# Attention in a streaming encoder step: the value products of a query row issued in one burst behind the step's scores and transposes

## The chip, the cores and the metric

The kernel runs on one core of one Trainium2 chip. The metric is the device time of one execution in microseconds (us). Three runs of the kernel before gave 3194.82, 3190.05 and 3192.64 us, so the median is 3192.64 us.

## The reference, cut to what matters

One layer of a hybrid encoder is computed for 2048 prompt frames and 32 sample frames: a mixer (projections and an RWKV recurrence), attention, an output projection with routing, a mixture of experts and a final normalization. The change is in the attention alone. For each of 8 heads, with blocks of 128 queries, it computes

```
s = q_nope . k_nope + q_pe . k_pe          # 96 channels
s = where(key chunk <= query chunk, s * MLA_SCALE, -inf)   # chunks of 64
p = softmax(s)                             # over all keys up to the query's block
out = p . v                                # 64 channels a head
```

All is float32.

## The kernel before, in words

Function `attention` (line 1265) works on two heads at a time (h = 0 and 1), so it makes four turns, one for each pair of heads. A turn first computes keys (L1546) and values (L1555) from the latents, ten groups in all, and then walks over 17 query rows j of 128 queries. Row j needs j + 1 key blocks; `groups(j)` (L1276) cuts them into groups of up to four blocks, so rows 0 to 3 have one group, rows 4 to 7 two, rows 8 to 11 three, rows 12 to 15 four. Row 16 holds the sample frames and has one group. A chunk is one group of one head: `chunks` (L1282) lists 82 of them in the order row, head, group. Chunk n goes through these stages:

- **scores** (L1491): TensorE multiplies queries by up to 512 keys into one of five PSUM banks (instruction L1497).
- **maxima** (L1582): VectorE takes the row maximum (L1593, the masked corner in L1589 or L1592); when the chunk is the last of its head in the row it also joins and scales the maxima (L1596, L1597).
- **exp** (L1469, corner L1472): ScalarE exponentiates. It needs the joined maximum of the row and head, so no chunk of a head can start before that head's last chunk has its maximum.
- **transposes** (L1500): TensorE turns the probabilities, up to four 128x128 blocks (L1509), into one of two PSUM banks (5 and 6).
- **copy**: VectorE copies the bank to one of 14 SBUF slots of `PT` (L1640).
- **value products** (`values`, L1512): for each pair of a row and a key block, both heads' products are accumulated in bank 7 (L1528). One such pair is four matmul records in the trace. The first product of row j waits for the output of row j - 1 (`out_{j-1}`), because both use bank 7.
- **row_sum** (L1599): VectorE adds the row sums of a head, inverts them and spreads them to 64 columns (L1602, L1603, L1609, tile `wide`). **row_rec** (L1534, called recT in the code) is one TensorE transpose of `wide` (L1537); it needs `wide` of both heads. ScalarE copies it out (L1482), and **output** (L1611) multiplies bank 7 by it (L1615).

The order is written out by hand. Every engine runs through numbered steps n and keeps its own program order. In step n TensorE issues `scores(n + 4)`, then the value products that the table `share` gives to the step, then `row_rec` if a row ends here (`row_end`), then `transposes(n)` (L1564 to L1572). VectorE issues `maxima(n + 4)`, then `row_sum` of chunk n - 2 where that is a head's last chunk, then `output` of the row that ended in step n - 1, then the copy of chunk n (L1625 to L1643). ScalarE issues `exp(n)`, then the copy of the row's reciprocals if a row ended in step n - 1.

The planner (L1295 to L1306) places each pair of a row and a key block not earlier than LAG = 3 steps after the second head's chunk of its group, with at most BURST = 3 pairs in a step, and starts a row at least two steps after the end of the row before:

```python
step = max(step, place[j, 1, g] + LAG, free)
while share.get(step, 0) == BURST:
    step += 1
```

A turn has 138 pairs. By this rule they fall into 52 steps of one to three pairs. For example, row 13 (14 pairs) is spread over five steps, and row 8 (9 pairs) over three.

Of the kernel before, what the change touches and what calls it, by code (L numbers as in the profile page):

```python
# [33 lines left out]
NT = SEQ // P + 1  # L34
# [1230 lines left out]
def attention(nc, io, scr):  # L1265
# [3 lines left out]
    KT = SEQ // P + 2  # L1269
    attnT = transposed_out(scr)  # L1270
    AHEAD, SB, TB = 4, 5, 2
    LAG = 3
    NP, NPT = 4, 14
    BURST = 3

    def groups(j):  # L1276
        if j == NT - 1:
# [5 lines left out]
    count = len(chunks)  # L1283
# [7 lines left out]
    def ends(n):  # L1291
        return n == count - 1 or chunks[n + 1][:2] != chunks[n][:2]
# [1 line left out]

    pairs = [(j, g, s) for j in range(NT) for g in range(len(groups(j))) for s in range(groups(j)[g][1])]  # L1295
    share, row_end = {}, {}
    step, free = 0, 0
    for i, (j, g, s) in enumerate(pairs):
        step = max(step, place[j, 1, g] + LAG, free)
        while share.get(step, 0) == BURST:  # L1300
            step += 1
        share[step] = share.get(step, 0) + 1
        if i + 1 == len(pairs) or pairs[i + 1][0] != j:
            row_end[step] = j
            free = step + 2
    steps = max(max(share) + 1, count)  # L1306
    last_use = {n: max(m for m in range(count) if m % NP == n % NP) for n in range(NP)}

    def in_order(ahead, before, at, after):
        names = [x for n in range(min(AHEAD, count)) for x in ahead(n)]  # L1310
        for n in range(steps):
            names += ahead(n + AHEAD) if n + AHEAD < count else []
            names += before(n) + (at(n) if n < count else []) + after(n)
        return names
# [14 lines left out]
        return [f"max{n}"] + ([f"rowmax{j}_{h}", f"negmax{j}_{h}"] if ends(n) else [])  # L1329

    def sum_names(n):
        if n < LAG - 1 or n - LAG + 1 >= count or not ends(n - LAG + 1):
            return []
        j, h, g = chunks[n - LAG + 1]
        return [f"sum{j}_{h}", f"sum_rec{j}_{h}", f"rec_wide{j}_{h}"]

    def out_names(n):
# [1 line left out]

    KV = [f"K{n}" for n in range(5)]  # L1340
    VV = [f"V{n}" for n in range(5)]
    ten_names = KV + VV + in_order(lambda n: [f"S{n}"], pv_names, lambda n: [f"PT{n}"], none)
    vec_names = VV + in_order(max_names, lambda n: sum_names(n) + out_names(n), lambda n: [f"PT{n}"], none)
    vec_names += out_names(steps)
    act_names = KV + [x for n in range(steps + 1) for x in
# [3 lines left out]
    with ExitStack() as ctx:  # L1349
# [136 lines left out]
        @block.tensor  # L1486
        def _(pe):
            pe.wait_ge(latents.sem, latents.done(0))
            pe.wait_ge(setup, 6)

            def scores(t, n):  # L1491
                j, h, gi = chunks[n]
                k0 = groups(j)[gi][0]
                wd, _ = width(n)
                if n >= SB:
                    t.w(act, f"exp{n - SB}")
                t.mark(pe.matmul(bank[n % SB][:, 0:wd], qT[h][keys(h), j * P:(j + 1) * P],  # L1497
                                 kT[h][keys(h), k0 * P:k0 * P + wd], start=True, stop=True), f"S{n}")

            def transposes(t, n):  # L1500
                wd, corner = width(n)
                t.w(act, f"exp{n}")
                if n >= TB:
                    t.w(vec, f"PT{n - TB}")
                if corner:
                    t.w(pol, f"corner{n}")
                for c in range(0, wd, P):
                    rows = min(P, wd - c)
                    ins = pe.transpose(bank[SB + n % TB][0:rows, c:c + P], PQ[:, n % NP, c:c + rows], ident[:, :])  # L1509
                t.mark(ins, f"PT{n}")  # L1510

            def values(t):  # L1512

                for j in range(NT):
                    gs = groups(j)
                    for gi, (k0, k, last) in enumerate(gs):
                        m0, m1 = place[j, 0, gi], place[j, 1, gi]
                        t.w(vec, f"PT{m1}")
                        if gi == 0:
                            if j > 0:  # L1520
                                t.w(vec, f"out_{j - 1}")
                            else:
                                t.w0(vec, last_out)
                        for s in range(k):
                            rows = last if s == k - 1 else P
                            end = gi == len(gs) - 1 and s == k - 1
                            for h, m in ((0, m0), (1, m1)):
                                ins = pe.matmul(bank[7][64 * h:64 * h + 64, 0:P], vals[0:rows, k0 + s, 64 * h:64 * h + 64],  # L1528
                                                PT[0:rows, m % NPT, s, :], start=(gi == 0 and s == 0), stop=end)
                            if s == k - 1:  # L1530
                                t.mark(ins, f"PV{j}_{gi}")
                            yield

            def row_rec(t, j):  # L1534

                t.w(vec, f"rec_wide{j}_1")
                t.mark(pe.transpose(bank[7][:, P:2 * P], wide[:].rearrange("p a n -> p (a n)"), ident[:, :]), f"recT{j}")  # L1537

            def turn(t):
                t.arrived(w_in)  # L1540
                t.w0(vec, last_out)
                t.w0(act, f"exp{count - 1}")
                for n in range(5):
                    wd = min(512, KT * P - 512 * n)
                    for c in range(CKV):
                        ins = pe.matmul(bank[n][:, 0:wd], w[:, c, 0:P], lat[:, c, 512 * n:512 * n + wd],  # L1546
                                        start=(c == 0), stop=(c == CKV - 1))
                    t.mark(ins, f"K{n}")
                for n in range(5):
                    b = bank[5 + n % 3]  # L1550
                    if n >= 3:
                        t.w(vec, f"V{n - 3}")
                    for k in range(4 * n, min(4 * n + 4, KT)):
                        for c in range(CKV):
                            ins = pe.matmul(b[:, (k % 4) * P:(k % 4 + 1) * P], lat[:, c, k * P:(k + 1) * P],  # L1555
                                            w[:, c, P:2 * P], start=(c == 0), stop=(c == CKV - 1))
                    t.mark(ins, f"V{n}")
                t.w(act, "K4")
                t.w(vec, "V4")
                t.arrived(q_in)  # L1560
                for n in range(AHEAD):
                    scores(t, n)
                v = values(t)
                for n in range(steps):  # L1564
                    if n + AHEAD < count:
                        scores(t, n + AHEAD)
                    for _ in range(share.get(n, 0)):
                        next(v)
                    if n in row_end:
                        row_rec(t, row_end[n])  # L1570
                    if n < count:
                        transposes(t, n)  # L1572
                for _ in v:
                    pass

            engine_loop(pe, ten, turns, turn)

        @block.vector
        def _(v):
# [37 lines left out]
            def turn(t):  # L1617
# [7 lines left out]
                for n in range(steps + 1):  # L1625
                    if n + AHEAD < count:
                        maxima(t, n + AHEAD)
                    if sum_names(n):
                        row_sum(t, n - LAG + 1)
                    if n - 1 in row_end:  # L1630
                        output(t, row_end[n - 1])
                    if n < count:
# [976 lines left out]
```

How the kernel before makes its waits and increments, by code:

```python
    def _wait(self, counts, name, turn):  # L199
        v = self.known.get((counts.sem.name, name, turn))
        if v is None:
            v = counts.done(self.i + turn, name) if name else counts.done(self.i + turn)
        self.eng.wait_ge(counts.sem, v)
# [1 line left out]
    def do(self, ins, name):  # L205
        self.own.mark(ins, name)
        self.eng.wait_ge(self.own.sem, self.own.done(self.i, name))
# [314 lines left out]
        @block.sync  # L523
# [11 lines left out]
                consts.go(sp.dma_start(w_wa[hs], io["w_wa"][hs, 512 * r:512 * r + 512]))  # L535
                consts.go(sp.dma_start(cst[hs], io["cst"].rearrange("p (a n) -> p a n", a=7)[hs, :, hs]))
                consts.go(sp.dma_start(one64[hs], io["ident"][hs, hs]))
                consts.go(sp.dma_start(levs[hs], io["levs"].rearrange("p (a n) -> p a n", a=LEVELS)
                                      [hs, 0:LEVELS - 1, 32 * r:32 * r + 32]))
            consts.go(sp.dma_start(w_g[:], io["w_g"]))
            for k in (1, 0, 2):
                c0, c1 = w_cols[k]
                sp.dma_start(w_in[:, :, c0:c1], w_src[:, :, c0:c1]).then_inc(w_part[k], 16)
            sp.dma_start(w_uq[:], io["w_uq"].rearrange("p (a n) -> p a n", a=CQ)).then_inc(w_queries, 16)
            sp.wait_ge(first_x, 2)
            def x_load(tile):
# [91 lines left out]
            for d in (mla_out, rwkv_out, edge_out, state_out):  # L640
                sp.wait_ge(d.sem, d.done(NT - 1))
            sp.wait_ge(x_in.sem, x_in.done(NT + 1))
# [805 lines left out]
        @block.scalar  # L1448
        def _(a):
            a.wait_ge(setup, 6)
            def turn(t):
```

## Time and profile before

| what | value |
|---|---|
| median of three runs | 3192.64 us |
| span of the profiled execution, first to last instruction | 3185.8 us |
| TensorE matmul busy over the span | 2883.6 us (91%) |
| VectorE busy over the span | 1738.2 us (55%) |
| mean granted TensorE clock | 0.965 of full speed |
| attention with its setup, all four turns | about 1378 to 2075 us from the span's start |

The profile of one execution gives no total beside its span; the 6.8 us between the span and the median lie around the span or between executions. In timelines a line gives the start in us, the duration in us, the engine, the line of the code, the operation, its output and inputs, and the count that is merged; a bracket at the end gives how long the engine stood idle before it and what released it. Ends of matmuls are modelled, so the distance from one start to the next start is the better measure of TensorE's time. In the four turns the first scores start at 1396.58, 1570.82, 1743.95 and 1917.87 us, and the turns follow each other in the same pattern, so the first turn is read.

### The profile page before, as it was taken

What the parts mean: (1) busy time and instruction counts of PE and PEld (TensorE: products, weight loads), DVE (VectorE), ACT (ScalarE), POOL (GpSimd) and SP (SyncE); (2) the same over time, 40 slices, a digit from 0 to 9 for tenths busy, and PEclk for the clock granted to TensorE, in tenths of its full rate; (3) what the DMA queues carried; (4) which work ended last, traced back from release to release, by engine and by line L of the source; (5) the groups of instructions that cost most, each with busy time, mean ns of one, the idle gap of its engine ahead of it and who ended that gap; (6) DMA issues with size and microseconds to landing.
All of it is one profiled execution on the core that took longest, in us unless ns stands there. A gap on an engine that the chain in (4) does not pass through costs nothing. (4 is left out here: it accounts for less than half of the span.)

```text
span 3185.8 us, 65923 instructions
## 1 busy us (share of the span) xinstructions
PE 2883.6 (91%) x26600; PEld 2202.1 (69%) x26600; DVE 1738.2 (55%) x3821; ACT 970.2 (30%) x2497; POOL 522.3 (16%) x554
## 2 busy tenths in 40 slices
PE   7999999999999999669899898989976999999990
PEld 6888888888888888545555555545545777777770
DVE  1666666666666666558686868822235222222225
ACT  2333333333333333234343434412220111111116
POOL 0000000000000000010000000011113554545540
PEclk9999999999999999689999999999988999999995
DMA  6211111222111211420101010033335899886447
GB/s 196 37 38 37 37 37 38 40 39 39 37 38 39 42 38 37 93 88 1 39 1 39 1 36 1 1 127 132 126 110 210 282 336 325 278 279 177 97 93 251
DMA packets 337225, 310.23 MB, mean 97 GB/s; under 512 B 235200, under 2 KB 290528, under 8 KB 322528
## 3 DMA queue, kind: packets, MB, share of 16 engines
q1 hardware_dynamic: 315424, 238.88, 24.5%
q0 software_dynamic: 21504, 67.13, 9.1%
q8 instruction: 218, 3.57, 0.5%
q14 instruction: 79, 0.65, 0.1%
HBM read 208.12 MB, written 84.42 MB: 92 GB/s over the span
## 5 line engine op out<-in xcount | busy, mean ns | idle before, releaser
L814 PE MATMUL mx_bank<-mx_xT,mx_w_in 128*128 128x128 f32 x5168 | 646.4, 281 | 16.9 <-DVEq L281 13.4
L814 PEld LDWEIGHTS mx_bank<-mx_xT,mx_w_in 128*128 128x128 f32 x5168 | 600.8, 193 | 60.5 <-issue 36.2
L2311 DVE STREAM_TRANSPOSE ex_xT<-ex_x 128x256 f32<-128x256 f32 x256 | 141.5, 610 | 332.3 <-DMA ex_x<-scr_hx,ex_idx 332.3
L1497 PE MATMUL at_bank<-pl_kT,pl_qT 128*128 128x512 f32 (+5 forms) x656 | 289.9, 528 | 2.3 <-issue 2.3
L1469 ACT ACTIVATE at_PQ<-at_bank,at_nms 128x512 f32<-128x512 f32 (+5 forms) x328 | 192.7, 595 | 252.9 <-DVE at_nms L1597 251.5
L2159 POOL DMA_INDIRECT ex_x<-scr_hx,ex_idx x256 | 244.9, 957 | 114.8 <-issue 77.7
L2242 PE MATMUL ex_gate<-pl_wg,ex_xT 128*128 x1024 | 233.6, 381 | 13.7 <-DVE ex_xT L2311 11.4
L2242 PEld LDWEIGHTS ex_gate<-pl_wg,ex_xT 128*128 128x128 f32 x1024 | 195.1, 191 | 68.7 <-issue 44.9
L2266 PE MATMUL ex_down<-pl_wd,ex_hT 128*128 x512 | 230.3, 592 | 1.5 <-ACT ex_hT L2194 1.5
L2242 PE MATMUL ex_up<-pl_wu,ex_xT 128*128 x1024 | 231.6, 379 | 0.0
L1528 PEld LDWEIGHTS at_bank<-at_PT,at_vals 128*64 128x64 f32 (+1 forms) x2208 | 117.4, 136 | 151.5 <-issue 78.1
L1640 DVE COPY at_PT<-at_bank 128x512 f32<-128x512 f32 (+3 forms) x328 | 196.4, 600 | 44.6 <-PE at_bank L1509 28.1
L2242 PEld LDWEIGHTS ex_up<-pl_wu,ex_xT 128*128 128x128 f32 x1024 | 190.2, 191 | 23.1
L2202 ACT ACTIVATE ex_y<-ex_down,kept_onehot 128x512 f32<-128x512 f32 x128 | 81.0, 684 | 410.6 <-PE ex_down L2266 410.6
L1509 PE MATMUL at_bank<-pl_at_ident,at_PQ 128*128 128x128 f32 x1104 | 184.9, 282 | 22.5 <-ACT at_PQ L1469 11.7
L710 ACT ACTIVATE mx_pr<-mx_bank 128x256 f32<-128x256 f32 (+1 forms) x68 | 36.7, 540 | 553.3 <-PE mx_bank L814 471.7
L1509 PEld LDWEIGHTS at_bank<-pl_at_ident,at_PQ 128*128 128x128 f32 x1104 | 126.4, 141 | 107.2 <-issue 44.6
L1593 DVE TENSOR_REDUCE at_mx<-at_bank 128x1 f32<-128x512 f32 (+5 forms) x328 | 188.6, 575 | 15.9 <-PE at_bank L1497 10.5
L1528 PE MATMUL at_bank<-at_PT,at_vals 128*64 128x128 f32 (+1 forms) x2208 | 165.8, 282 | 26.1 <-DVE at_o_sb L1615 26.1
L665 POOL TENSOR_TENSOR mx_AR<-mx_u,mx_ep 128x512 f32<-128x512 f32 x17 | 20.1, 1181 | 1000.2 <-DVE mx_kh L1154 1000.2
L2266 PEld LDWEIGHTS ex_down<-pl_wd,ex_hT 128*128 128x128 f32 x512 | 97.2, 190 | 96.8 <-issue 93.6
L2170 POOL DMA_INDIRECT scr_acc<-ex_y,kept_tokens x64 | 103.3, 1615 | 271.1 <-ACT ex_y L2202 128.9
(310 smaller groups left out, 4480.2 us busy)
## 6 DMA issues: line engine op xcount, KB each, us to landing
pl_wg<-in_w_eg SPq DMA_DIRECT2D x32, 1024.0 KB, 6.1
pl_wu<-in_w_eu SPq DMA_DIRECT2D x32, 1024.0 KB, 10.3
pl_wd<-in_w_ed SPq DMA_DIRECT2D x32, 1024.0 KB, 14.3
mx_x<-in_x SPq DMA_DIRECT2D x76, 128.0 KB, 3.7
pl_ro_x<-in_x SPq DMA_DIRECT2D x17, 512.0 KB, 4.2
scr_hx<-ro_h SPq DMA_DIRECT2D x17, 512.0 KB, 2.6
scr_acc<-ro_ha SPq DMA_DIRECT2D x17, 512.0 KB, 3.1
co_r<-scr_acc SPq DMA_DIRECT2D x17, 512.0 KB, 5.6
```

Of the source, the lines that this page charges most:

```text
L814: ins = pe.matmul(dst, w_in[:, k, col:col + n], xT[:, k, :], start=(k == 0), stop=(k == KC - 1))
L1469: ins = a.activation(PQ[:, n % NP, 0:full], b[:, 0:full], ACT.Exp, bias=bias, scale=SCALE, accum_out=sums[:, j, h, 1 + gi:2 + gi])
L1497: t.mark(pe.matmul(bank[n % SB][:, 0:wd], qT[h][keys(h), j * P:(j + 1) * P], kT[h][keys(h), k0 * P:k0 * P + wd], start=True, stop=True), f ...
L1509: ins = pe.transpose(bank[SB + n % TB][0:rows, c:c + P], PQ[:, n % NP, c:c + rows], ident[:, :])
L1528: ins = pe.matmul(bank[7][64 * h:64 * h + 64, 0:P], vals[0:rows, k0 + s, 64 * h:64 * h + 64], PT[0:rows, m % NPT, s, :], start=(gi == 0 an ...
L1593: t.do(v.tensor_reduce(mx[:, 1 + gi:2 + gi], b[:, 0:wd], AX.X, ALU.max), f"max{n}")
L1640: ins = v.tensor_copy(PT[:, n % NPT, 0:full, :], b[:, 0:full * P].rearrange("p (a n) -> p a n", a=full))
L2159: x_in[s].go(g.indirect_dma_start(x[s][:, k, :], None, rows, bass.IndirectOffsetOnAxis(ap=idx[:, at:at + 1], axis=0)))
L2170: y_add[s].go(g.indirect_dma_start(scr["acc"], bass.IndirectOffsetOnAxis(ap=tokens[:, at:at + 1], axis=0), y[s][:], None, compute_op=ALU.add))
L2242: ins = pe.matmul(b[s][:, 0:FE], xT[s][:, k, :], wv[:, k * FE:(k + 1) * FE], start=(k == 0), stop=(k == KC - 1))
L2266: ins = pe.matmul(down_b[n][:, :], hT[s][:, m, :], wv[:, m * D + n * 512:m * D + (n + 1) * 512], start=(m == 0), stop=(m == FC - 1))
L2311: ins = v.transpose(xT[s][:, :, 32 * h:32 * h + 32], x[s][:, h, :].rearrange("p (i k) -> p k i", k=KC))
```

## The change

The planner places whole rows. A row with one, two or three groups has all its value products in one step, LAG = 2 steps after the last chunk of the row; a row with four groups has two such steps, one for its first two groups (8 pairs), one for the rest. In the step the value products now come behind the transposes. The number of the chunk whose sum VectorE takes in step n stays n - 2.

```diff
-    LAG = 3
+    LAG = 2
     NP, NPT = 4, 14
-    BURST = 3
...
-    step, free = 0, 0
-    for i, (j, g, s) in enumerate(pairs):
-        step = max(step, place[j, 1, g] + LAG, free)
-        while share.get(step, 0) == BURST:
-            step += 1
-        share[step] = share.get(step, 0) + 1
-        if i + 1 == len(pairs) or pairs[i + 1][0] != j:
-            row_end[step] = j
-            free = step + 2
+    free = 0
+    for j in range(NT):
+        gs = groups(j)
+        parts = ((0, 1), (2, 3)) if len(gs) == 4 else (tuple(range(len(gs))),)
+        for part in parts:
+            step = max(place[j, 1, part[-1]] + LAG, free)
+            assert step not in share
+            share[step] = sum(gs[g][1] for g in part)
+            free = step + 1
+        row_end[step] = j
+        free = step + 2
...
-        if n < LAG - 1 or n - LAG + 1 >= count or not ends(n - LAG + 1):
+        if n < LAG or n - LAG >= count or not ends(n - LAG):
...
                     if n + AHEAD < count:
                         scores(t, n + AHEAD)
+                    if n < count:
+                        transposes(t, n)
                     for _ in range(share.get(n, 0)):
                         next(v)
                     if n in row_end:
                         row_rec(t, row_end[n])
-                    if n < count:
-                        transposes(t, n)
...
-                        row_sum(t, n - LAG + 1)
+                        row_sum(t, n - LAG)
```

A turn then has 21 steps with value products instead of 52. They are steps 3, 5, 7 and 9 (rows 0 to 3, 1 to 4 pairs), 13, 17, 21 and 25 (rows 4 to 7, 5 to 8 pairs), 31, 37, 43 and 49 (rows 8 to 11, 9 to 12 pairs), 55 and 57, 63 and 65, 71 and 73, 79 and 81 (rows 12 to 15, 8 pairs and then 5 to 8), and 83 (row 16, 2 pairs). Before, rows 0 to 15 ended in steps 4, 6, 8, 11, 14, 18, 23, 27, 32, 39, 45, 51, 59, 67, 75 and 84.

## Rows read from the trace of the kernel before

**Rows 1.** The profile's page: span, and busy time of two engines

```profile
span 3185.8 us, 65923 instructions
...
PE 2883.6 (91%) x26600; PEld 2202.1 (69%) x26600; DVE 1738.2 (55%) x3821; ACT 970.2 (30%) x2497; POOL 522.3 (16%) x554
```

**Rows 2.** Busy time by stretch: bounds, us, PE, PEld, DVE, ACT, POOL, clock, DMA, GB/s

```profile
1396.60:1443.60 47.00, 39.45 (x247) 23.21 (x248) 41.81 (x150) 22.98 (x87) 3.69 (x13) 0.96 0.03 7
1443.60:1485.30 41.70, 40.42 (x291) 24.49 (x290) 36.10 (x99) 19.14 (x69) 1.99 (x7) 1.00 0.00 1
1485.30:1539.80 54.50, 51.88 (x379) 30.28 (x377) 44.58 (x109) 21.16 (x74) 1.99 (x7) 1.00 0.00 1
1539.80:1552.70 12.90, 9.37 (x101) 6.62 (x99) 8.47 (x32) 4.68 (x17) 1.35 (x5) 0.99 0.56 131
...
1412.00:1416.00 4.00, 4.00 (x19) 2.50 (x19) 3.64 (x15) 1.75 (x7) 0.28 (x1) 0.57 0.00 0
```

**Rows 3.** VectorE's timeline, first 47 us: its two longer waits

```profile
1421.60 0.69 DVE L1640 COPY at_PT<-at_bank 128x512 f32<-128x512 f32 x1 [0.92 <-PE at_bank L1509]
...
1428.60 0.69 DVE L1640 COPY at_PT<-at_bank 128x512 f32<-128x512 f32 x1 [0.41 <-DVE at_mx L1593]
```

**Rows 4.** TensorE's timeline: a step without value products, one with three pairs

```profile
1471.90 1.02 PE L1497 MATMUL at_bank<-pl_kT,pl_qT 96*128 96x512 f32 x2
...
1473.20 1.02 PE L1497 MATMUL at_bank<-pl_kT,pl_qT 128*128 128x512 f32 x2
...
1476.64 1.02 PE L1497 MATMUL at_bank<-pl_kT,pl_qT 128*128 128x512 f32 x2
...
1478.90 1.02 PE L1497 MATMUL at_bank<-pl_kT,pl_qT 96*128 96x512 f32 x2
```

**Rows 5.** TensorE's timeline: a burst of one pair, transposes ahead of value products

```profile
1442.64 0.44 PE L1528 MATMUL at_bank<-at_PT,at_vals 128*64 128x128 f32 x4
1443.01 0.33 PE L1537 MATMUL at_bank<-pl_at_ident,at_wide 128*128 128x128 f32 x1
...
1542.61 0.63 PE L1509 MATMUL at_bank<-pl_at_ident,at_PQ 128*128 128x128 f32 x4 [0.51 <-DVE at_PT L1640]
```

**Rows 6.** Timeline of all engines, turn's end: TensorE's longest burst

```profile
1543.17 0.88 PE L1528 MATMUL at_bank<-at_PT,at_vals 128*64 128x128 f32 x12
...
1547.60 1.75 PE L1528 MATMUL at_bank<-at_PT,at_vals 128*64 128x128 f32 x28
...
1549.28 0.33 PE L1537 MATMUL at_bank<-pl_at_ident,at_wide 128*128 128x128 f32 x1
```

**Rows 7.** VectorE's timeline: reciprocals of rows 1 and 5, and the next full maximum

```profile
1410.80 0.26 DVE L1609 TENSOR_SCALAR at_wide<-at_ones,at_rec 128x64 f32<-128x64 f32 x1
...
1411.63 0.68 DVE L1593 TENSOR_REDUCE at_mx<-at_bank 128x1 f32<-128x512 f32 x1
...
1434.41 0.25 DVE L1609 TENSOR_SCALAR at_wide<-at_ones,at_rec 128x64 f32<-128x64 f32 x1
...
1435.05 0.68 DVE L1593 TENSOR_REDUCE at_mx<-at_bank 128x1 f32<-128x512 f32 x1
```

**Rows 8.** Timeline of all engines, steps 67 and 68: a head's chain

```profile
1522.48 0.81 PE L1497 MATMUL at_bank<-pl_kT,pl_qT 128*128 128x384 f32 x2
...
1524.61 0.69 ACT L1469 ACTIVATE at_PQ<-at_bank,at_nms 128x512 f32<-128x512 f32 x1 [4.92 <-DVE at_nms L1597]
...
1525.44 0.66 PE L1509 MATMUL at_bank<-pl_at_ident,at_PQ 128*128 128x128 f32 x4
```

**Rows 9.** TensorE's timeline: waits for row 6's output and for an exp

```profile
1446.58 0.88 PE L1528 MATMUL at_bank<-at_PT,at_vals 128*64 128x128 f32 x12 [1.28 <-DVE at_o_sb L1615]
...
1488.38 0.66 PE L1509 MATMUL at_bank<-pl_at_ident,at_PQ 128*128 128x128 f32 x4 [1.30 <-ACT at_PQ L1469]
```

**Rows 10.** TensorE's timeline inside the stretch of lower clock

```profile
1413.95 1.91 PE L1497 MATMUL at_bank<-pl_kT,pl_qT 96*128 96x512 f32 x2
```

More of the change, by code:

```diff
@@ L1331, in sum_names @@
     def sum_names(n):
-        if n < LAG - 1 or n - LAG + 1 >= count or not ends(n - LAG + 1):
+        if n < LAG or n - LAG >= count or not ends(n - LAG):
             return []
-        j, h, g = chunks[n - LAG + 1]
+        j, h, g = chunks[n - LAG]
         return [f"sum{j}_{h}", f"sum_rec{j}_{h}", f"rec_wide{j}_{h}"]
@@ L1341, in attention @@
     VV = [f"V{n}" for n in range(5)]
-    ten_names = KV + VV + in_order(lambda n: [f"S{n}"], pv_names, lambda n: [f"PT{n}"], none)
+    ten_names = KV + VV + in_order(lambda n: [f"S{n}"], none, lambda n: [f"PT{n}"], pv_names)
     vec_names = VV + in_order(max_names, lambda n: sum_names(n) + out_names(n), lambda n: [f"PT{n}"], none)
```

## The prediction

> **What bounds the kernel now.** The page comes first: TensorE is busy 91% of the span, VectorE 55% [rows 1]. That is an average over stages; the change touches only the part of attention in which chunks are processed, four times some 156 us. I therefore cut the first turn by the rows that are worked on. Rows 0 to 7 (steps 0 to 23) take 47.0 us, with VectorE busy 41.81 us in 150 instructions [rows 2]. Its timeline has only two idle gaps worth the name there, 0.92 and 0.41 us [rows 3]; the rest of the difference are hundredths between its instructions. So VectorE is the bound of the short rows. In rows 8 to 11 (41.7 us) and in steps 48 to 75 (54.5 us) it is TensorE: busy 40.42 and 51.88 us, against 36.10 and 44.58 for VectorE [rows 2].
>
> **What TensorE pays for a burst.** A full step without value products takes 1473.20 - 1471.90 = 1.30 us from scores to scores, one with three pairs 1478.90 - 1476.64 = 2.26 us [rows 4]. So three pairs cost 0.96 us. One pair takes 0.37 us from its first product to the reciprocals' transpose [rows 5], seven pairs 1.68 us [rows 6]: a pair costs (1.68 - 0.37) / 6 = 0.218 us. Three pairs are 0.65 us of work, and 0.31 us is the price of a burst as such, the two switches of operand shape. Behind transposes the entry takes 1543.17 - 1542.61 = 0.56 us [rows 5, 6], where four transposes ahead of scores take 0.44 (1.30 less 0.86 for the scores), so 0.12 us. The exit into scores doesn't occur in this trace. Its nearest row is the exit into the reciprocals' transpose, 0.37 - 0.22 = 0.15 us, and I add 0.07 us for the slower first weights, which gives 0.34 us a burst; the bounds are 0.2 and 0.5 us, or 3 us either way in a turn of 21 bursts.
>
> **The parts of the change, per turn.** The operations stay the same in number and shape, and no DMA moves. 52 bursts become 21. If TensorE were the bound throughout, that would give 52 x 0.31 - 21 x 0.34 = 9.0 us a turn. What remains of it, stretch by stretch:
>
> *Rows 0 to 7: loss.* Here the order matters, not the count. VectorE forms the reciprocals of a row in step n by chunk n - 2, as before. TensorE's transpose of them stood one step later; now, with LAG = 2, it stands in the same step n, ahead of scores n + 5. Behind the waiting transpose are queued those scores, for which VectorE waits in its next step. Before, they were already in their bank. VectorE is behind TensorE here, so the wait is real. Take row 1: the reciprocals end at 1410.80 + 0.26 = 1411.06 and the next full maximum started at 1411.63 [rows 7]. Now the transpose (0.07 us to reach it, 0.17 us itself) and the scores (1.02 us, 0.08 us to VectorE) lie between: 1411.06 + 1.34 = 1412.40, which is 0.77 us later. Row 5: 1434.66 + 1.34 = 1436.00 against 1435.05, 0.95 us. The other six row ends read in the same way give 1.10, 0.47, 1.02, 1.09, 0.08 (a narrow chunk) and 0.82 us, and the 0.92 and 0.41 us gaps [rows 3] are taken off rows 3 and 4. Together +5.0 us. Bounds: 1 us, if TensorE turns out to be less ahead, and 7 us.
>
> *Rows 8 to 11: gain.* 14 bursts become 4: 14 x 0.31 - 4 x 0.34 = 3.0 us. The 1.28 us wait for row 6's output [rows 9] goes too, since the next row's products now come four steps behind. But a burst of 8 to 11 pairs holds back the next scores by 2.1 to 2.7 us, and VectorE, whose own work is only 3 to 4 us shorter than the stretch, then runs dry; afterwards TensorE waits for its copies. Laid out by hand with the durations above (0.72 us a maximum, 0.60 us a copy, 0.55 us a row sum), I find 0.3 to 0.7 us a row, some 2.4 us in all. Net -1.9 us; bounds -4 and 0.
>
> *Steps 48 to 75: nothing.* 19 bursts become 7: 19 x 0.31 - 7 x 0.34 = 3.5 us. Against it stands the chain of a head. The first transposes of head 1 in a row of four groups need an exp, it needs the joined maximum, and that needs the head's last scores, issued only one step before. From those scores to the transposes it took 1525.44 - 1522.48 = 2.96 us [rows 8]. TensorE's own work between them was the two pairs, the reciprocals' transpose and two groups of scores, and it stood still for some 0.3 us; in the three such places of this stretch 0.27, 0.31 and 0.52 us. In the new order there is no burst between them: 0.86 + 0.44 + 0.86 = 2.16 us of cover, and VectorE comes out of the preceding burst late, so the wait is about 1.2 us, +2.5 us for three rows. The 1.30 us wait at the first head of row 12 [rows 9] grows to about 2.3 us, because its scores also follow a VectorE that is behind. Net 0; bounds -3 and +2.
>
> *The end of the turn.* Steps 76 to 83 take 12.9 us [rows 2]. Before, nine pairs filled waits between the last transposes; now two bursts of 8 come whole, 8 x 0.218 + 0.34 = 2.1 us each, the second behind all transposes, as the burst of seven was [rows 6]. One wait more for head 1, one switch less: +0.5 us, bounds -0.5 and +1.5.
>
> *The clock.* From 1412 to 1416 us the granted clock was 0.57 on average, that is mostly the lower level of 1.2 GHz, after a stretch in which TensorE worked only now and then [rows 2]. The scores took 1.91 instead of 1.02 us [rows 10, 4]. This cost little, because VectorE was the bound; now scores are on the chain. I take half such a case a turn, +0.4 us.
>
> **The sum.** 5.0 - 1.9 + 0 + 0.5 + 0.4 = 4.0 us a turn, 16 us over four. The profiled span of 3185.8 us [rows 1] becomes 3202; the median of the runs lies 6.8 us above the span, and with that unchanged the time is 3208.5 us, 0.5% slower. Within 0.2% (6.4 us) a measurement of this kernel can't tell a difference from none.
>
> **The rivals.**
> *Faster: the price of the switches decides.* Its place is steps 24 to 75, where TensorE is the bound. If VectorE has enough in hand to bridge the bursts, the two stretches give 3.0 + 1.3 + 3.5 = 7.8 us instead of 1.9; if at the same time the transpose's wait costs only 3 us in the short rows, a turn gains 7.8 - 3 - 0.5 - 0.4 = 3.9 us: 3177 us. For it speaks TensorE's 97% and 95% in those stretches, and that transposes now reach VectorE ahead of the products. Against it speaks how near VectorE's own sum lies. It decides once the losses (5.0 + 2.4 + 3.5 + 0.5 + 0.4 = 11.8 us a turn in my sum) stay under 7.8 - 1.6 = 6.2 us. Chance 0.24.
> *No difference.* The short rows lose 3 us rather than 5, because TensorE, also held up by whole bursts, is less ahead, and the long rows give 2 to 3 us: 3190 to 3199 us. Chance 0.20.
> *Slower by much: the clock falls in the short rows.* TensorE has less to do per us there than now, and steps without value products are scores and transposes alone. At the lower level each of eight row ends costs 1.91 - 1.02 = 0.89 us more, 7 us a turn, less the 0.4 counted: 3235 us. Against it: the last stretches, with steps that hold no products too, stood at 1.00 [rows 2]. Chance 0.08.
> The Trainium skill (TensorE: Matmul & The Clock Gate, Part 4: PE-mode transpose) says that transposes do not count as activity for the clock. By that rule even the long rows' steps of scores and transposes would be at risk, and the clock case more likely. The trace doesn't bear it out so far, the clock of 1.00 in steps 24 to 75 being the number beside it.
> That bursts would be split again can be left aside: every copy that a burst needs lies at least two steps behind, and the tables are fixed.
>
> **How the numbers follow.** The forecast, 3199 to 3225 us, has 0.48, with the clock case on its side 0.56 for slower. Faster has 0.24, the same 0.20. Single terms at their bounds move the sum by up to 4 x 4 us down and 4 x 3 us up. The range from 3184 to 3228 us holds the forecast, the case without a difference and the nearer part of the faster one; it leaves out about 0.12 below and 0.08 above.
>
> **What would show it.** In rows 0 to 7 VectorE's maxima should wait 0.5 to 1 us for scores once per row, TensorE's transpose of the reciprocals should wait for `wide`, and the stretch should grow from 47 to about 52 us. Steps 24 to 47 should shrink to about 40 us, with no wait for outputs. Waits of TensorE's transposes for exps should be above 1 us once in each of rows 12 to 15. If the transpose of the reciprocals finds them ready in the short rows, the forecast is wrong, and so is its sign; if steps 24 to 75 come to under 91 us instead of 94, the hand-laid waits were too large.

## The result and the profile after

Four runs of the changed kernel gave 3217.28 to 3222.66 us, median 3219.36. Four runs of the kernel before beside them gave a median of 3191.41 us. The ratio is 1.0091, with a 95% interval from 1.0076 to 1.0105: the change costs 28 us, where 16 were forecast. Most of it, but not all, is the wait that the prediction put first.

The page of the kernel after: the span and the busy time of the engines, then from its costliest groups the maxima (instructions | busy, mean ns | idle time ahead of them, and what ended it). From L1300 on, the line numbers are those of before plus one.

```profile
span 3217.1 us, 65943 instructions
...
PE 2873.3 (89%) x26600; PEld 2222.9 (69%) x26600; DVE 1735.1 (54%) x3821; ACT 973.4 (30%) x2497; POOL 522.4 (16%) x554
...
L1594 DVE TENSOR_REDUCE at_mx<-at_bank 128x1 f32<-128x512 f32 (+5 forms) x328 | 188.4, 574 | 74.1 <-PE at_bank L1498 70.5
```

The work is the same (26600 matmul records both times, VectorE busy 1735.1 against 1738.2 us [rows 1]), and the span is 31.3 us longer. VectorE's maxima now stand idle for 70.5 us behind TensorE's scores. The four turns start at 1396.02, 1577.17, 1759.17 and 1940.07 us, on average 181.35 us apart instead of 173.76: a turn lost 7.6 us. This distance between turns is the measure that I use for the experiments as well, since it comes from three turns of one trace. Four times what a kernel has lost or gained in it against the kernel before is the change in time to within some 3 us. Part of that uncertainty is the clock: the stretch from step 76 of a turn to the first scores of the next, with the same work each time, took 31.02 and 31.14 us at granted clocks of 0.94 and 0.95 in the kernel before, and 29.45 us at 1.00.

The first turn of the kernel after, cut at the same steps as [rows 2], with the same columns; then the two pieces of its beginning in which the clock was low:

```profile
1396.00:1449.30 53.30, 41.58 (x248) 25.34 (x249) 42.25 (x151) 23.28 (x88) 3.70 (x13) 0.90 0.03 6
1449.30:1489.80 40.50, 38.17 (x290) 25.15 (x289) 35.70 (x96) 19.02 (x68) 2.00 (x7) 1.00 0.00 1
1489.80:1545.20 55.40, 48.65 (x378) 31.72 (x377) 42.65 (x107) 21.77 (x74) 1.99 (x7) 1.00 0.00 1
1545.20:1558.90 13.70, 8.78 (x100) 6.72 (x99) 9.60 (x36) 4.55 (x16) 1.32 (x5) 1.00 0.52 124
...
1407.00:1411.00 4.00, 3.96 (x13) 2.44 (x15) 1.95 (x7) 2.42 (x9) 0.07 (x1) 0.50 0.00 0
1411.00:1418.00 7.00, 5.95 (x33) 4.00 (x33) 4.79 (x20) 2.18 (x7) 0.50 (x2) 0.61 0.00 0
```

Rows 0 to 7 took 53.3 us (before 47.0), rows 8 to 11 40.5 (41.7), steps 48 to 75 55.4 (54.5), the end 13.7 (12.9). In the second and third stretch TensorE is busy 38.17 and 48.65 us, 2.3 and 3.2 us less than before: the saved switches are really there. But the stretches shrink by only 1.2 us, and grow by 0.9. Half of TensorE's saved work in the second stretch, and all of it in the third, has become waiting.

TensorE's timeline in rows 0 to 3, after. L1538 is the transpose of the reciprocals, and the bracket gives how long TensorE stood before it:

```profile
1406.96 0.48 PE L1538 MATMUL at_bank<-pl_at_ident,at_wide 128*128 128x128 f32 x1 [3.15 <-DVE at_wide L1610]
1407.23 1.92 PE L1498 MATMUL at_bank<-pl_kT,pl_qT 96*128 96x512 f32 x2
...
1412.69 0.47 PE L1538 MATMUL at_bank<-pl_at_ident,at_wide 128*128 128x128 f32 x1 [0.67 <-DVE at_wide L1610]
...
1418.55 0.33 PE L1538 MATMUL at_bank<-pl_at_ident,at_wide 128*128 128x128 f32 x1 [0.93 <-DVE at_wide L1610]
...
1423.55 0.33 PE L1538 MATMUL at_bank<-pl_at_ident,at_wide 128*128 128x128 f32 x1 [0.97 <-DVE at_wide L1610]
```

VectorE's timeline after, the maxima that follow these scores (rows 0 to 5):

```profile
1409.18 0.69 DVE L1594 TENSOR_REDUCE at_mx<-at_bank 128x1 f32<-128x512 f32 x1 [1.95 <-PE at_bank L1498]
...
1414.91 0.69 DVE L1594 TENSOR_REDUCE at_mx<-at_bank 128x1 f32<-128x512 f32 x1 [1.81 <-PE at_bank L1498]
...
1419.78 0.69 DVE L1594 TENSOR_REDUCE at_mx<-at_bank 128x1 f32<-128x512 f32 x1 [0.69 <-PE at_bank L1498]
...
1424.78 0.69 DVE L1594 TENSOR_REDUCE at_mx<-at_bank 128x1 f32<-128x512 f32 x1 [1.08 <-PE at_bank L1498]
...
1432.45 0.69 DVE L1594 TENSOR_REDUCE at_mx<-at_bank 128x1 f32<-128x512 f32 x1 [0.95 <-PE at_bank L1498]
...
1440.52 0.69 DVE L1594 TENSOR_REDUCE at_mx<-at_bank 128x1 f32<-128x512 f32 x1 [0.82 <-PE at_bank L1498]
```

The two engines take turns, once in each of rows 0 to 5: TensorE waits for the reciprocals, and VectorE for the scores that are queued behind them. In rows 0 and 1 the wait is twice as long, since the scores themselves took 1.92 us at the lower clock.

TensorE's timeline in the long rows, after: two waits for an exp, and between them a whole burst of eight pairs and the steps behind it.

```profile
1492.86 0.66 PE L1510 MATMUL at_bank<-pl_at_ident,at_PQ 128*128 128x128 f32 x4 [2.02 <-ACT at_PQ L1470]
...
1505.95 1.97 PE L1529 MATMUL at_bank<-at_PT,at_vals 128*64 128x128 f32 x32
1507.85 1.13 PE L1498 MATMUL at_bank<-pl_kT,pl_qT 128*128 128x512 f32 x2
1508.82 0.66 PE L1510 MATMUL at_bank<-pl_at_ident,at_PQ 128*128 128x128 f32 x4
...
1510.17 0.60 PE L1510 MATMUL at_bank<-pl_at_ident,at_PQ 128*128 128x128 f32 x4
1510.70 1.31 PE L1529 MATMUL at_bank<-at_PT,at_vals 128*64 128x128 f32 x20
...
1516.66 0.66 PE L1510 MATMUL at_bank<-pl_at_ident,at_PQ 128*128 128x128 f32 x4 [1.57 <-ACT at_PQ L1470]
```

The burst's price can be read here. Its entry is 1510.70 - 1510.17 less the 0.44 of four transposes, 0.09 us; its exit is 1507.85 - 1505.95 less 8 x 0.218, 0.16 us; and the scores behind it take 0.97 us to the next transposes instead of 0.86, another 0.11 us. Together 0.36 us, where 0.34 was assumed.

The totals of three waits over all four turns, after (us, times, longest); in the kernel before they were, in the same order, 10.5, 11.7 and 10.1 us:

```profile
DVE at_mx L1594 <- PE at_bank L1498: 70.5, 68, 2.4
...
PE at_bank L1510 <- ACT at_PQ L1470: 36.6, 32, 2.0
PE at_bank L1538 <- DVE at_wide L1610: 34.0, 28, 3.2
```

### The profile page after: what moved, and what is told of

Read it like the earlier page. It is cut to its first block and busy times, and to the rows that moved or that the text cites. A ratio compares the mean times of both kernels' runs of the same rounds, so it can differ in the third digit from the quotient of the medians.

```text
span 3217.1 us, 65943 instructions
## 1 busy us (share of the span) xinstructions
PE 2873.3 (89%) x26600; PEld 2222.9 (69%) x26600; DVE 1735.1 (54%) x3821; ACT 973.4 (30%) x2497; POOL 522.4 (16%) x554
## 5 line engine op out<-in xcount | busy, mean ns | idle before, releaser
L1510 PEld LDWEIGHTS at_bank<-pl_at_ident,at_PQ 128*128 128x128 f32 x1104 | 136.5, 144 | 215.3 <-ACT at_PQ L1470 98.7
L1594 DVE TENSOR_REDUCE at_mx<-at_bank 128x1 f32<-128x512 f32 (+5 forms) x328 | 188.4, 574 | 74.1 <-PE at_bank L1498 70.5
L1529 PE MATMUL at_bank<-at_PT,at_vals 128*64 128x128 f32 (+1 forms) x2208 | 144.9, 283 | 6.9 <-DVE at_o_sb L1616 3.6
L1445 POOL TENSOR_TENSOR at_PQ<-at_zero 64x64 f32<-64x64 f32 x128 | 36.0, 285 | 676.4 <-PE at_bank L1510 676.3
```

Of the source, the lines that this page charges most:

```text
L1594: t.do(v.tensor_reduce(mx[:, 1 + gi:2 + gi], b[:, 0:wd], AX.X, ALU.max), f"max{n}")
```

## The experiments

Three causes could share the 28 us. *The wait* (W in the expectations): the transpose of the reciprocals stands in the step of its sum, ahead of the next scores. *The cover* (C): in the rows of four groups no value products stand between a head's last scores and the transposes that need them. *The placement* (P): value products behind the transposes cost something by themselves, whatever their number. And a part of the first could be the clock. Each kernel below was timed beside the kernel before on the same chip; the ratio is to that, with its 95% interval.

| kernel | median us | ratio | turn to turn, us |
|---|---|---|---|
| before | 3188.6 to 3193.3 | 1 | 173.8 |
| after | 3219.4 | 1.0091 [1.0076, 1.0105] | 181.3 |
| e1 before, whole bursts only | 3194.5 | 1.0023 [1.0014, 1.0033] | 174.9 |
| e2 before, behind the transposes only | 3210.3 | 1.0068 [1.0051, 1.0084] | 179.8 |
| e3 before, LAG = 2 only | 3232.6 | 1.0139 [1.0122, 1.0156] | 185.3 |
| e4 after, reciprocals late | 3192.1 | 1.0010 [1.0000, 1.0020] | 174.6 |
| e5 after, cover | 3204.8 | 1.0044 [1.0030, 1.0058] | 177.8 |
| e8 after, both | 3181.4 | 0.9968 [0.9955, 0.9980] | 171.9 |
| e6 after, 22 matmuls | 3226.4 | 1.0114 [1.0097, 1.0131] | 183.3 |
| e7 after, 22 transposes | 3218.1 | 1.0084 [1.0068, 1.0101] | 180.9 |
| e9 after, 11 matmuls | 3219.6 | 1.0090 [1.0070, 1.0110] | 180.2 |
| e10 e1 with cover | 3185.2 | 0.9985 [0.9976, 0.9995] | 173.1 |
| e11 e8, row 11 split | 3172.8 | 0.9941 [0.9924, 0.9957] | 168.6 |
| e12 e4 with bursts of three | 3204.0 | 1.0037 [1.0023, 1.0051] | 176.9 |

**One part of the change alone.** Three kernels each make one part of the change to the kernel before.

e1, the new planner, with LAG = 3 and the products ahead of the transposes:

```diff
-    BURST = 3
...
-        while share.get(step, 0) == BURST:
-            step += 1
...
+            step = max(place[j, 1, part[-1]] + LAG, free)
```

> The kernel before with the new planner alone: whole-row bursts, but LAG stays 3, the reciprocals' transpose stays one step behind its row sum, and the value products stay ahead of the transposes. If the transpose's wait in the short rows is the cause (theory W), rows 0 to 7 stay at 47 to 48.5 us a turn, and the kernel lies between the two: about 3195 us (3188 to 3203). If the length of the bursts is the cause (rival S), it is as slow as the changed kernel or slower, because here VectorE also waits for transposes behind each burst: 3215 us or more.

3194.46 us, as expected. No wait for the reciprocals is added (12.1 us in all, before 10.1), but transposes wait for exps: TensorE's timeline of e1, the first and the second head of row 12 (the second heads of rows 13 and 14 wait 1.14 and 0.96 us).

```profile
1488.03 0.66 PE L1510 MATMUL at_bank<-pl_at_ident,at_PQ 128*128 128x128 f32 x4 [2.01 <-ACT at_PQ L1470]
1496.83 0.66 PE L1510 MATMUL at_bank<-pl_at_ident,at_PQ 128*128 128x128 f32 x4 [1.33 <-ACT at_PQ L1470]
```

So whole bursts bring next to nothing by themselves: 52 bursts became 21, but steps 24 to 75 shrink only by 1.6 us in the first turn (40.6 and 54.1 us, before 41.7 and 54.5), because the waits come with the bursts and not with the place behind the transposes. That the turn is 1.1 us longer all the same comes from its other parts: the end of the first turn took 13.95 us (before 12.9), and the later turns' ends with the next keys and values had a lower clock (0.95 and 0.90, before 1.00 and 0.95).

e2, the new order with the old planner:

```diff
+                    if n < count:
+                        transposes(t, n)
                     for _ in range(share.get(n, 0)):
                         next(v)
                     if n in row_end:
                         row_rec(t, row_end[n])
-                    if n < count:
-                        transposes(t, n)
```

> The kernel before with the value products and the reciprocals' transpose moved behind the step's transposes; LAG 3 and bursts of up to three pairs stay. Theory W: the transpose still has one step of slack, so no loss in the short rows, and VectorE gets its transposes earlier: 3183 to 3192 us. Rival S: bursts are as short as before, so no change either. If the place behind the transposes itself costs (rival P), 3200 us or more.

Missed: 3210.29 us. I had expected next to nothing of the placement, and it costs 6.0 us a turn. TensorE's timeline of e2 in steps with three pairs each:

```profile
1518.56 0.66 PE L1509 MATMUL at_bank<-pl_at_ident,at_PQ 128*128 128x128 f32 x4 [0.88 <-ACT at_PQ L1469]
...
1519.95 1.12 PE L1497 MATMUL at_bank<-pl_kT,pl_qT 128*128 128x512 f32 x2
...
1522.25 1.13 PE L1497 MATMUL at_bank<-pl_kT,pl_qT 128*128 128x512 f32 x2
```

Its steps 48 to 75 in the first turn, with the columns of [rows 2]:

```profile
1484.97:1542.95 57.98, 53.24 (x379) 31.79 (x378) 43.77 (x110) 21.15 (x74) 2.27 (x8) 1.00 0.00 1
```

The step itself is hardly dearer: 1522.25 - 1519.95 = 2.30 us against 2.26 in [rows 4]. The loss is in the long rows, where steps 48 to 75 grew by 3.4 us and rows 8 to 11 by 1.3 us, while rows 0 to 7 took 45.9 us, 1.1 less than before. Products between scores and transposes gave VectorE and ScalarE time for maximum and exp; behind the transposes they hold back the next scores instead. Each of the four first heads of rows 12 to 15 now waits for an exp, 1.90, 0.94, 0.88 and 0.71 us, where the kernel before has 1.30 and 0.31 us in rows 12 and 13, none in 14 and 15, and 0.27 and 0.52 us at the second heads of rows 12 and 13. VectorE's maxima waited 48.2 us for scores over the four turns (before 10.5), but e4 below has 49.9 us of the same wait and loses next to nothing, so this total is no price. The same placement with whole bursts doesn't show the cost: e1 has the products ahead of the transposes, e4 behind, and their turns differ by 0.3 us. And e12 below, with bursts of three behind the transposes but LAG = 2 and the late reciprocals, is 3.1 us a turn above the kernel before, not 6.0. Why the price differs between the two isn't tested; that with few bursts most steps have no products to put on either side is an argument.

e3, LAG = 2 with the sums left at chunk n - 2, and nothing else:

```diff
-    LAG = 3
+    LAG = 2
...
-                        row_sum(t, n - LAG + 1)
+                        row_sum(t, n - LAG)
```

> The kernel before with LAG = 2 alone (row sums still by chunk n - 2), so that the reciprocals' transpose comes in the step of its row sum, for rows 0 to 3 and wherever the bursts of three allow it. Theory W: rows 0 to 3 lose some 3 us a turn as in the changed kernel, the later rows little because their last burst of three falls some steps later: 3200 to 3208 us. Rivals S and P: no loss, 3188 to 3194 us.

3232.60 us, more than expected and more than the whole change. TensorE's timeline of e3, row 1:

```profile
1411.95 0.48 PE L1537 MATMUL at_bank<-pl_at_ident,at_wide 128*128 128x128 f32 x1 [0.68 <-DVE at_wide L1609]
1412.22 0.85 PE L1509 MATMUL at_bank<-pl_at_ident,at_PQ 128*128 128x128 f32 x3
1412.86 1.92 PE L1497 MATMUL at_bank<-pl_kT,pl_qT 128*128 128x512 f32 x2
```

Behind the wait stand the step's transposes as well as the next scores, so VectorE waits for both: 25.2 us for scores and 52.0 us for the transposes that it copies (before 10.5 and 28.1). Rows 0 to 7 took 55.2 us, 8.2 more than before, and 1.9 more than in the change, where the transposes are issued before the wait. So their new place seems to soften what LAG = 2 does; the two kernels also differ in their bursts, and no run changes that place alone.

**The wait.** e4 is the changed kernel with the transpose of the reciprocals one step later, behind the next scores:

```diff
                     if n + AHEAD < count:
                         scores(t, n + AHEAD)
+                    if n - 1 in row_end:
+                        row_rec(t, row_end[n - 1])
...
-                    if n in row_end:
-                        row_rec(t, row_end[n])
```

> The changed kernel with the reciprocals' transpose alone moved one step later, behind the next scores. Theory W: rows 0 to 7 fall from 53.3 to about 47.5 us a turn, the clock's dip there gets shorter, the other stretches stay: 3219 - 4 x 6 = 3195 us (3190 to 3200). Rival S: little is gained, 3212 us or more.

3192.09 us: of the 28 us this one move gives back 26 by the ratios and 27 by the turns (6.8 us each). Its rows 0 to 7, with the columns of [rows 2], and TensorE's timeline in rows 1 and 2:

```profile
1395.65:1443.17 47.52, 41.68 (x247) 24.20 (x248) 41.93 (x151) 23.23 (x88) 3.70 (x13) 0.93 0.03 7
...
1410.36 2.07 PE L1502 MATMUL at_bank<-pl_kT,pl_qT 128*128 128x512 f32 x2
1412.23 0.42 PE L1542 MATMUL at_bank<-pl_at_ident,at_wide 128*128 128x128 f32 x1
...
1416.53 0.28 PE L1542 MATMUL at_bank<-pl_at_ident,at_wide 128*128 128x128 f32 x1
```

The scores are ahead, and the transpose finds its input ready. From row 1's to row 2's it takes 4.30 us, against 5.86 in the kernel after. Averaged over three turns, rows 0 to 7 took 47.0 us before, 53.1 after and 47.3 in e4: so 5.7 of the 6.8 us lie where the wait was. In the first turn's short rows one wait of VectorE's full maxima for scores is left, 1.79 us in row 1. The rest of the 6.8 us is a balance of other parts. Steps 48 to 75 took 1.1 us more than after (57.1 us in the second and third turn, with clocks of 0.97 there, 55.4 in the first, at 1.00), and the end with the next keys and values 1.9 us less.

**The cover.** e5 issues the second burst of rows 12 to 15 two steps later, where head 1 of the next row has its chain:

```diff
-            step = max(place[j, 1, part[-1]] + LAG, free)
+            step = max(place[j, 1, part[-1]] + LAG + (2 if part == (2, 3) else 0), free)
```

> The changed kernel with the second burst of each row of four groups two steps later, so that it stands between the last scores of head 1 and that head's first transposes. In the changed kernel those transposes wait 1.76, 1.57, 1.39 and 1.79 us a turn for the exp. If the chain of a head is a cost of its own (theory C), the waits go, a turn gains 3 to 4 us and the kernel comes to 3219 - 14 = 3205 us (3201 to 3209). If VectorE's total work sets the pace there and the wait only shows its lag (rival V), less than 4 us is gained, 3215 us or more.

> Both repairs: the reciprocals' transpose one step later, behind the next scores, and the second burst of long rows two steps later. If the two causes are apart and add up, 3192 - 14 = 3178 us (3172 to 3184), below the kernel before, because only now the saved switches of operand shape are left over. Rival V: 3189 to 3193 us.

e5 took 3204.78 us, and e8, which is e4 and e5 together, 3181.35 us, faster than the kernel before. TensorE's waits for exps in e5 are 0.32 us (row 13), none (row 14) and 0.25 (row 15) instead of 1.57, 1.39 and 1.79. The gains are 6.8 and 3.5 us a turn alone, and 9.4 together: two causes, nearly independent. What was left in the long rows of e8 are above all the two waits of row 12, since row 11 ahead of it has its products in one burst. TensorE's timeline of e8:

```profile
1488.84 0.66 PE L1514 MATMUL at_bank<-pl_at_ident,at_PQ 128*128 128x128 f32 x4 [1.90 <-ACT at_PQ L1474]
...
1498.01 0.66 PE L1514 MATMUL at_bank<-pl_at_ident,at_PQ 128*128 128x128 f32 x4 [1.02 <-ACT at_PQ L1474]
```

e11 therefore splits row 11 too: the four pairs of its first group in step 47, the other eight in step 51, where all twelve stood in step 49:

```diff
-        parts = ((0, 1), (2, 3)) if len(gs) == 4 else (tuple(range(len(gs))),)
+        parts = ((0, 1), (2, 3)) if len(gs) == 4 else ((0,), (1, 2)) if j == 11 else (tuple(range(len(gs))),)
...
-            step = max(place[j, 1, part[-1]] + LAG + (2 if part == (2, 3) else 0), free)
+            step = max(place[j, 1, part[-1]] + LAG + (2 if part in ((2, 3), (1, 2)) else 0), free)
```

> The late transpose and the covered chain, and row 11's products in two bursts at steps 47 and 51, between the last scores of row 12's two heads and their first transposes. Those two transposes still wait 1.90 and 1.02 us a turn for exps. Theory C: 2 to 2.5 us a turn go, 3181 - 9 = 3172 us (3169 to 3177). Rival V (VectorE's own work sets the pace there, which has more to do in rows 8 to 11 than TensorE): 3178 us or more.

3172.76 us, 0.9941 [0.9924, 0.9957] of the kernel before. In TensorE's timeline of e11 row 12 has one wait left, and the next is row 13's of 0.28 us:

```profile
1489.02 0.66 PE L1514 MATMUL at_bank<-pl_at_ident,at_PQ 128*128 128x128 f32 x4 [0.68 <-ACT at_PQ L1474]
```

By the medians this kernel beats both, by 17 and by 47 us. e10 takes the same cover to e1, the products ahead of the transposes and the second burst one step later:

> The kernel before with whole-row bursts (LAG 3, value products ahead of the transposes, so the reciprocals' transpose has a step of slack) and the second burst of a long row moved to the step of head 1's last scores. The same two repairs as in the fastest version so far, by another way. Theory (both causes are all there is): 3194 - 12 = 3182 us (3178 to 3187). If the place ahead of the transposes starves VectorE behind bursts of 8 to 12 pairs, 3190 us or more.

3185.23 us, as expected: 1.8 us a turn better than e1. Both orders gain from the cover.

**What the bursts are worth.** e12 is e4 with the old planner's bursts of up to three pairs (LAG = 2):

> The changed kernel with the late reciprocals' transpose, but with the old planner's bursts of up to three pairs (52 steps a turn instead of 21; LAG 2). It tells what the size of the bursts is worth once the transpose waits no longer. If the saved switches count in full where TensorE is the bound (31 bursts a turn at 0.37 us, two thirds of them in rows 8 to 15), it is some 25 us above the whole-row version with the late transpose: 3212 us or more. If long bursts starve VectorE by as much as they save, and the short ones cover the head chains, it equals it: 3188 to 3196 us.

3204.01 us, between the two theories. Whole bursts are worth 2.3 us a turn, or 9 us by the ratios. By counting switches they would be worth 31 x 0.36 = 11 us a turn. By stretches of the first turn the gain is in rows 8 to 11, 40.3 us in e4 against 42.9 in e12; steps 48 to 75 are level (55.4 and 55.2), and rows 0 to 7 nearly so (47.5 and 48.0). The rest is paid back or worth nothing from the start: e12's waits for exps in the long rows are only 0.58, 0.67, 0.71 and 0.72 us, where e4 with its whole bursts has 1.90, 1.02, 0.94 and 0.85, and in the short rows VectorE is the bound.

**The clock.** Three kernels put useless work into step 3, just ahead of the wait of 3.15 us in row 0, into an unused part of bank 7. They add this, with `pe.transpose` in e7, and 11 instead of 22 in e9; nobody reads the result.

```diff
+                    if n == 3:
+                        for _ in range(22):
+                            pe.matmul(bank[7][:, 2 * P:3 * P], ident[:, :], ident[:, :], start=True, stop=True)
                     if n in row_end:
                         row_rec(t, row_end[n])
```

> The changed kernel with 22 more 128x128 matmuls of no use (their result is read by nobody) in step 3, in the 3.15 us in which TensorE waits for the reciprocals of row 0; by 0.109 us each they fill 2.4 us of it. If the lower clock in the rows behind costs time because TensorE stood idle before (theory K), the granted clock stays at 1.00 through rows 0 to 2, and a turn gains 1 to 2 us: 3212 to 3216 us. If the clock is no cost there, 3219 us as before.

> The same with 22 transposes in place of the matmuls, of the same time by their rows. If transposes count as TensorE's activity like matmuls, the same clock and time as with matmuls (3212 to 3216 us); if they do not, as the Trainium skill says (TensorE: Matmul & The Clock Gate, Part 4: PE-mode transpose), the clock falls as in the changed kernel: 3219 us.

> The changed kernel with 11 useless matmuls in step 3 in place of the 22 of the run before it: a float32 matmul of 128 columns took 0.228 us there, a transpose 0.119, so 11 of them fill the same 2.5 us as the 22 transposes did. It is read by the clock, not by the time. If only the length of the filled time counts, the clock behaves as with the transposes: one dip of some 3.4 us in rows 1 to 2 of a turn. If matmuls count for more than transposes (the skill's rule), there is no dip in rows 0 to 2, as with 22 matmuls. Time in either case 3212 to 3220 us.

e6 missed because of its own filler: a matmul was two records and took 5.18 / 22 = 0.24 us, a transpose 2.62 / 22 = 0.12, so the filler overran the wait, and row 0's reciprocals came 1.8 us late. By row 3 that was made up (27.41 us after the turn's first scores, after 27.53), with a clock of 1.00 in these rows. What e6 lost it lost in the long rows: its steps 48 to 75 took 58.5 us instead of 55.4, with spells of lower clock that the kernel after doesn't have there (0.94 on average), and so it was in every turn (57.0 to 58.5 us).

```profile
1488.78:1547.29 58.51, 51.77 (x378) 33.85 (x377) 42.66 (x107) 21.74 (x74) 1.99 (x7) 0.94 0.01 1
```

TensorE's timelines: e6's and e7's filler, then e9's and the transposes of reciprocals of rows 0 to 3.

```profile
1402.82 5.18 PE L1574 MATMUL at_bank<-pl_at_ident 128*128 128x128 f32 x44
```

```profile
1401.88 2.62 PE L1574 MATMUL at_bank<-pl_at_ident 128*128 128x128 f32 x22
```

```profile
1405.66 2.72 PE L1574 MATMUL at_bank<-pl_at_ident 128*128 128x128 f32 x22
1408.89 0.33 PE L1538 MATMUL at_bank<-pl_at_ident,at_wide 128*128 128x128 f32 x1 [0.50 <-DVE at_wide L1613]
1413.75 0.33 PE L1538 MATMUL at_bank<-pl_at_ident,at_wide 128*128 128x128 f32 x1 [1.14 <-DVE at_wide L1613]
1418.61 0.33 PE L1538 MATMUL at_bank<-pl_at_ident,at_wide 128*128 128x128 f32 x1 [1.05 <-DVE at_wide L1613]
1423.61 0.33 PE L1538 MATMUL at_bank<-pl_at_ident,at_wide 128*128 128x128 f32 x1 [0.97 <-DVE at_wide L1613]
```

e9 is the clean one. Its filler lies wholly in the wait: row 0's reciprocals come 10.94 us after the turn's first scores (1397.95), exactly as in the kernel after (1406.96 - 1396.02). The stretches of e9 and of e7, with the columns of [rows 2], have this clock:

```profile
1407.00:1411.00 4.00, 3.49 (x24) 2.52 (x22) 2.83 (x11) 1.69 (x6) 0.00 (x0) 1.00 0.00 0
1411.00:1418.00 7.00, 4.23 (x35) 2.67 (x33) 5.72 (x23) 2.91 (x11) 0.57 (x2) 1.00 0.01 2
```

```profile
1407.00:1411.00 4.00, 2.09 (x13) 1.21 (x13) 3.08 (x14) 1.45 (x6) 0.28 (x1) 0.86 0.00 0
1411.00:1418.00 7.00, 5.91 (x34) 3.85 (x32) 4.78 (x17) 3.43 (x13) 0.28 (x1) 0.84 0.01 2
```

With the matmuls in the wait the clock stood at 1.00 where it had been 0.50 and 0.61, that is mostly 1.2 GHz. The rows followed each other after 4.86, 4.86 and 5.00 us instead of 5.73, 5.86 and 5.00. So the lower clock costs 1.9 us of the turn's beginning. The time didn't follow, though: 3219.6 us for e9 and 3218.1 us for e7 can't be told from 3219.4 us, and the turns of e9 are only 1.2 us shorter on average. The third and the fourth again had a spell of lower clock in their first rows, from about 1773 and 1954 us on, and in the first and the third one came up in steps 48 to 75, which took 57.0 and 56.9 us there instead of 55.4:

```profile
1489.88:1546.92 57.04, 50.29 (x378) 32.56 (x377) 42.67 (x107) 21.73 (x74) 1.99 (x7) 0.97 0.00 1
```

With transposes as filler for almost the same 2.6 us (e7) the clock fell later and for a shorter time, and row 1 kept its 5.86 us.

The Trainium skill (TensorE: Matmul & The Clock Gate, Part 4: PE-mode transpose) says that a transpose does not count as busy time of TensorE in the way that other matmuls do. The pair e7 and e9 leans to it, with 0.84 against 1.00 from 1411 to 1418 us. But transposes did delay the fall: over rows 0 to 7 the clock was 0.97 in all four turns of e7, 1.00, 1.00, 0.97 and 0.97 in e9, and 0.90, 0.90, 0.93 and 0.93 without a filler. No run settles it.

## Why the prediction was right, and which terms were off

The sign and the order of the causes were right. The time lies 11 us above the forecast and inside the range. By its own steps, for the first turn:

- *Rows 0 to 7, +5.0 for the order and +0.4 for the clock; measured +6.3 together.* The mechanism is shown by e4. The waits of VectorE in rows 0 to 5 are 1.95, 1.81, 0.69, 1.08, 0.95 and 0.82 us, predicted as 1.10, 0.77, 0.47, 1.02, 1.09 and 0.95. The excess of 1.9 us in the first two is the lower clock, and e9, without it, runs these rows 1.9 us faster. So the order costs 4.4 us and **the clock 1.9 us, which was mis-sized at 0.4**. I had taken half a case because VectorE had hidden such a stretch before [rows 2]; but the change itself makes the wait for row 0's reciprocals, ahead of the fall, longer (3.15 us, before 2.30) and puts the scores on the chain just there, for two rows. As e6 and e9 show, these 1.9 us are the clock's cost in this place and not what the whole time gains without it.
- *Rows 8 to 11, -1.9; measured -1.2.* TensorE stands still for 40.50 - 38.17 = 2.3 us in place of 1.3 [rows 2], 2.2 us of it in four transposes that wait for VectorE's copy, as the 2.4 us laid out by hand had it, and the 1.28 us wait for row 6's output [rows 9] is gone. What fell short is the busy time, 2.3 us less instead of 3.0, for which I have no test.
- *Steps 48 to 75, 0; measured +0.9.* The waits are 2.02, 1.76, 1.57 and 1.39 us (first head of row 12, second heads of rows 12 to 14) against 1.30, 0.27, 0.31 and 0.52 in time order before, that is +4.3 us. I had +3.5, with 1.2 us for each second head. I had also taken all of 0.27, 0.31 and 0.52 for waits of second heads; the 0.31 is the first head of row 13, and the second head of row 14 had none. The gain of the bursts, predicted at 3.5 us, is 51.88 - 48.65 = 3.2 us of busy time. e5 and e11 show that these waits are on the path: where they go, the time goes.
- *The end, +0.5; measured +0.8,* with a wait of 1.79 us for head 1 of row 15 in it.
- *The price of a burst, 0.34; measured 0.36.* The 0.07 us in it for slower first weights stood on no row; what came there is 0.11 us on the scores behind the burst.
- *What would show it:* the stretches came to 53.3 us (about 52 said) and 40.5 (about 40), each of rows 12 to 15 had its wait above 1 us, and steps 24 to 75 took 95.9 us, nowhere near the 91 that would have spoken against the waits.
- *The sum, +4.0 a turn; measured +6.8 in the first turn, and +7.6 from turn to turn.* By the starts of the turns it is +6.9, +8.9 and +7.0. What the second has beyond the others is from its step 76 to the next turn's scores, 32.54 us against 29.45: the clock was 0.90 there, and 1.00 in the kernel before. The sum had no term for the clock outside the short rows.

The rival "faster, the price of the switches decides" fell by the point it had named: the losses had to stay under 6.2 us a turn, and rows 0 to 7 alone lost 6.3. e12 shows that, even with the wait gone, whole bursts bring 2.3 us a turn instead of 7.8. "The clock falls in the short rows" was half right, in its place and its kind, but in two rows of eight, not in all. What the prediction didn't see was the price of the placement alone (e2). In the change it was covered by the whole bursts, so no term of the sum was wrong by it; but the text's remark that the transposes now reach VectorE earlier was counted for the change, and with bursts of three the same move costs 6 us a turn in e2.

## What to carry to other kernels

Price a moved instruction by what is queued behind it on its engine and who waits for that: one transpose of 0.17 us, moved back by one step, gave the short rows 5.7 us a turn, 23 of the 28 us; what the long rows lost in cover and gained in switches nearly cancelled. With the step's transposes queued behind it as well (e3) the short rows lost still more. Read such a gain in the stretch where it should lie, since spells of lower clock elsewhere move a turn by 1 to 3 us. Short pieces of independent work between the two ends of a dependence are cover, even if each costs a switch; collect them into bursts only after finding what covers the chain instead, and place a burst inside the longest chain (e8, e11: together with the wait mended, 1.0091 became 0.9941).

## What the runs showed of the hardware

- A float32 matmul of 128 columns with 128x128 weights ran as two records and took 0.24 us (5.18 us for 22), a transpose of the same size as one record 0.12 us (2.62 us for 22). That was the fault in e6.
- Full scores right behind a burst of products took 0.97 us to the next transposes, 0.86 us otherwise.
- A spell of 1.2 GHz that was driven out of one place of a turn by work in the wait turned up in others: steps 48 to 75 had clocks of 0.94 (e6) and 0.97 (e9) and took 3.1 and 1.6 us longer than at 1.00. The cost in one place, 1.9 us, was not the gain in the time.
